# One looped copy in place of three nested copies of the code for an expert's further token blocks

## What is computed

```python
def moe_ffn(h, w_router, b_router, w_gate, w_up, w_down):
    expert, weight = group_limited_route(h, w_router, b_router)
    ...
    counts = jnp.bincount(e_flat, length=N_EXPERTS)
    padded = (counts + MOE_BLOCK - 1) // MOE_BLOCK * MOE_BLOCK
    ...
    def expert_block(args):
        tok, e = args
        xb = h[tok]
        return (jax.nn.silu(xb @ w_gate[e]) * (xb @ w_up[e])) @ w_down[e]
    y = lax.map(expert_block, (tok_buf.reshape(n_blocks, MOE_BLOCK), blk_exp))
```

## Time and profile before

| what | value |
|---|---|
| median of 3 runs | 1489.23 us (1488.87 to 1491.04) |
| span of the profiled execution | 1493.5 us |
| PE busy | 1380.9 us (92%), 7075 matmuls |
| DVE busy | 982.7 us (66%) |
| ACT busy | 726.7 us (49%) |
| experts of layer 0, of layer 1 | about 445 to 750 us, about 1137 to 1472 us |
| packets of the first instruction queue (q8) | 54, 0.88 MB |

### The profile page before, as it was taken

One profiled execution on the slowest core, in us unless ns is written; L12 is line 12 of the kernel. 1 busy time (PEld: TensorE's weight loads), 2 busy tenths in 40 slices (PEclk: granted clock), 3 DMA queues, 4 the chain that ended last, 5 costly groups with the idle time before them and its releaser, 6 DMA issues.

```text
span 1493.5 us, 18753 instructions
## 1 busy us (share of the span) xinstructions
PE 1380.9 (92%) x7075; PEld 1091.2 (73%) x7076; DVE 982.7 (66%) x934; ACT 726.7 (49%) x776; POOL 296.3 (20%) x255
## 2 busy tenths in 40 slices
PE   3999999999988999999949999999998899999893
PEld 1776877666866788888748787788777688888582
DVE  4324575323487899998971657632757889999285
ACT  4324355122254777766642635522325677776260
POOL 1000000000024344555310000000013435444130
PEclk9999999999999999999969999999998999999997
DMA  9766302776675999999743130132364899999365
GB/s 298 273 225 228 139 1 85 247 259 204 229 280 208 359 373 384 383 375 373 280 132 113 57 113 1 57 113 76 122 238 171 300 355 372 377 376 382 141 246 196
DMA packets 157267, 341.37 MB, mean 229 GB/s; under 512 B 17150, under 2 KB 19394, under 8 KB 157186
## 3 DMA queue, kind: packets, MB, share of 16 engines
q1 hardware_dynamic: 141170, 316.97, 58.7%
q0 software_dynamic: 16016, 23.30, 4.6%
HBM read 350.68 MB, written 23.61 MB: 251 GB/s over the span
## 4 chain that ended last, share of the span: by engine, by line
PE 76%; DVE 8%; DMA 6%; ACT 3%; DVEq 3%; issue 2%; SPq 2%; POOL 0%; ACTq 0%; POOLq 0%
PE PS L1185 15%; PE PS L1187 14%; PE PS L1186 14%; PE PS L1583 7%; PE PS L1587 7%; PE PS L1579 7%; PE PS L1119 3%; PE PS L1567 2%; DMA ring<-in_w_down 2%; ACT reg L939 1%; DVE ring_parts L2195 1%; DMA y_rows<-reg,icur 1%; PE PS L1592 1%; SPq L475 1%; DMA ring<-in_w_ada 1%
## 5 line engine op out<-in xcount | busy, mean ns | idle before, releaser
L1185 PE MATMUL PS<-ring_parts 128*128 128x512 f32 (+1 forms) x704 | 277.0, 393 | 8.8 <-DVE hT_parts L1827 5.1
L2195 DVE TENSOR_TENSOR ring_parts<-ring,reg_parts 128x2048 fp32r<-128x2048 f32 x124 | 278.2, 2285 | 7.5 <-ACT reg_parts L1043 7.4
L1043 ACT ACTIVATE reg_parts<-ring 128x2048 fp32r<-128x2048 f32 x124 | 230.6, 1909 | 82.3 <-DMA ring<-in_w_down 45.4
L1819 DVE TENSOR_TENSOR ring_parts<-ring,ring_parts 128x2048 fp32r<-128x2048 f32 (+1 forms) x52 | 112.9, 2210 | 153.9 <-ACT ring_parts L861 153.8
L1185 PEld LDWEIGHTS PS<-ring_parts 128*128 128x128 f32 x704 | 133.7, 190 | 60.1 <-issue 27.6
L861 ACT ACTIVATE ring_parts<-ring 128x2048 fp32r<-128x2048 f32 (+1 forms) x52 | 93.4, 1845 | 152.8 <-DMA ring<-in_w_in 113.9
L2195 DVE TENSOR_TENSOR ring_parts<-ring,hT_parts 128x2048 fp32r<-128x2048 f32 x68 | 155.3, 2289 | 11.1 <-issue 10.4
L1186 PE MATMUL PS<-hT_parts,ring_parts 128*128 128x512 f32 x384 | 150.4, 392 | 0.0
L1187 PE MATMUL PS<-ring_parts 128*128 128x512 f32 x384 | 150.4, 392 | 0.0
L1043 ACT ACTIVATE hT_parts<-ring 128x2048 fp32r<-128x2048 f32 x68 | 126.5, 1908 | 14.6 <-DMA ring<-in_w_gate 9.4
L1587 PE MATMUL PS<-ring_parts,reg_parts 128*128 128x512 f32 x528 | 130.6, 389 | 0.0
(11 more groups left out here) (328 smaller groups left out, 2398.6 us busy)
## 6 DMA issues: line engine op xcount, KB each, us to landing
ring<-in_w_up SPq DMA_DIRECT2D x32, 2048.0 KB, 17.4
ring<-in_w_gate SPq DMA_DIRECT2D x32, 2048.0 KB, 12.6
ring<-in_w_down SPq DMA_DIRECT2D x32, 2048.0 KB, 18.7
ring<-in_w_ada SPq DMA_DIRECT2D x40, 1024.0 KB, 5.3
ring<-in_w_in SPq DMA_DIRECT2D x16, 2048.0 KB, 7.8
ring<-in_w_ada SPq DMA_DIRECT2D x4, 2048.0 KB, 13.9
ring<-in_w_out SPq DMA_DIRECT2D x4, 2048.0 KB, 7.8
reg<-y_rows SPq DMA_DIRECT2D x16, 512.0 KB, 6.1
```

Of the source, the lines that this page charges most:

```text
L1043: act.activation(high[:, cols], ring[:, 3 * k + part, cols], ACT.Copy).then_inc(w_hi[part], 1)
L1185: pe.matmul(out_, left[0], right[0], start=first, stop=False)
L1819: tt(ring_r[:, unit_slot(n), cols], w, ring_r[:, 2 + n % 2, cols].bitcast(F32), ALU.subtract).then_inc(lo_done, 1)
L2195: tt(ring_r[:, 3 * k + part, cols], ring[:, 3 * k + part, cols], high[:, cols].bitcast(F32), ALU.subtract).then_inc(w_lo[part], 1)
```

## The change

`repeated_overflow_blocks` is new. It loads the count as before, tests once whether it is over 128, and inside that test runs a loop over b = 1, 2, 3 with b in a register; each pass compares the count with 128 b and runs `body` if it is larger. The code of `body` stands once at every call. PE, ACT and DVE call it; POOL keeps `overflow_blocks`. The bodies are unchanged: PE, ACT and DVE don't use the block's number.

```diff
+        def repeated_overflow_blocks(eng, e, done, body):
+
+            count = eng.value_load(cnt_i[0:1, bass.ds(e, 1)], min_val=0, max_val=SEQ)
+            with eng.If(count > P):
+                with eng.Fori(1, NT) as b:
+                    with eng.If(count > b * P):
+                        eng.reg_add(done, done, 1)
+                        body(None, eng.snap(done, min_val=1, max_val=4096))
+                        eng.nop()
+                eng.nop()
...
-                    overflow_blocks(act, e, done, body)
+                    repeated_overflow_blocks(act, e, done, body)
...
-                    overflow_blocks(pe, e, done, body)
+                    repeated_overflow_blocks(pe, e, done, body)
...
-                    overflow_blocks(dve, e, done, body)
+                    repeated_overflow_blocks(dve, e, done, body)
```

## The result

| | before | after |
|---|---|---|
| median of the runs of one comparison (16 each), us | 1491.72 (1486.74 to 1498.33) | 1485.45 (1481.22 to 1488.67) |
| ratio after to before | | 0.9946, 95% interval 0.9932 to 0.996 |
| the profiled execution: its time; span, us | as shown above; 1493.5 | 1481.74; 1480.1 |
| mean granted clock of TensorE in it | 0.969 | 0.973 |

The changed kernel is faster by 0.54%, which is 8.0 us (6.0 to 10.1). In all comparisons of this study together the kernel before has a mean of 1493.8 us over 103 runs and the changed kernel 1485.3 over 37: 8.5 us, with some 1.2 us either way from the spread of the runs (they come from several chips, so this is a summary and no comparison of its own).

What follows compares the result with a forecast made beforehand. PE, busy for 92% of the span, was taken as the bound. The terms 2.7 + 4.5 + 0.4 - 1.4 - 0.9 gave 5.3 us less, from 1489.2 to 1483.9 us; range 1481.5 to 1489.0.

Steps and rivals of the forecast that it cites:

- term (a): Ways around the bodies on PE in each layer's first steps: four holes go, 2.7 us less layer 0, 4.5 layer 1.
- of the window the trace disagrees: Loop over experts on PE: five blocks of code ran without one packet, against the skill's two-page window.
- term (b): Branch around the bodies in step 15 of layer 0, 4.9 us long: 0.4 us of its hold on PE go.
- term (c): Way out of expert 13's second block, layer 1: PE's remaining loop passes cost 1.4 us more (bounds 0.9 and 2.1).
- term (d): PE's clock behind expert 13's second block: longer idle may lengthen the low grant, 0.9 us more.
- Both cases that I named: Low-clock stretch behind expert 13's second block: 3.4 us longer, costing 1.7 us of work, or no longer, costing nothing.
- Weights take it back: In both layers PE's earlier start ends in waits for the down weights: 0.3 us less, 1488.9; chance 0.12.
- No effect on a first visit: A first visit costs a fetch however near the target; holes stay, way out is added: 1490.6 us; chance 0.07.
- The short loop misses its own code: After expert 13's block, four jumps of the further-block loop each cost a fetch: 7.9 us more, 1497.1; chance 0.08.

Runs made afterwards that it cites:

- Padding: The changed kernel with 308, 154 or 200 instructions behind PE's loop that never run; ratios to the kernel before 1.0028, 0.9988 and 0.9933.
- the engines one at a time: The changed kernel with the loop on PE alone, ratio to before 0.9953, or on ACT and DVE alone, 1.0008; the other engines keep three nested copies.
- the announced branch: The kernel before, with PE's branch around the bodies in steps 1 to 15 announced to the instruction fetch; 1490.85 us, ratio to before 0.998.
- 154 instructions never run: The changed kernel with 154 instructions behind PE's loop that a branch always skips; 1491.6 us, ratio to the kernel before 0.9988.
- the 308 run: The changed kernel with 308 instructions behind PE's loop that a branch always skips; 1496.59 us, ratio to the kernel before 1.0028.
- The six passes: The changed kernel with block numbers 1 to 6 in the loop in place of 1 to 3; 1489.9 us, ratio to the kernel before 0.9973.
- the counted loop: The changed kernel with the loop's end worked out once from the count, without comparisons inside; 1481.04 us, ratios to before 0.9921, 0.9926, 0.993.
- 200 never run: The changed kernel with 200 instructions behind PE's loop that a branch always skips; 1483.69 us, ratio to the kernel before 0.9933.

## Why the prediction was right, and where it was short

**The holes, term (a).** Right in cause and place. All four are gone, q8 brought 44 packets as forecast, no branch is over 0.35 us. Padding, the engines one at a time and, in layer 1, the announced branch show that it is the block in which the branch lands, and not the number of copies. The wording needs one correction: a target one block ahead is not free in itself (up to 2.2 us of branch with 154 instructions never run, and 2.4 with a hole of 1.4 at step 2 of layer 0 before); it is mostly short enough for PE's queue.

The Trainium skill (Runtime: NRT & Kernel Launch, Instruction fetch mechanics) forces a fetch where the target of a taken branch is outside a two-page window. For a first visit the runs agree in the main: 0.2 to 2.4 us of branch at one block ahead, 3.3 us and more at two. For code visited before they don't: the loops of this study, up to five blocks long, ran on without a packet. The same section also gives TensorE an instruction memory of 2048 instructions, eight of these blocks, in which such a loop fits. So the prediction's "of the window the trace disagrees" holds against the section's two pages, and not against that figure; no run here has a loop long enough to test it.

The size was short. I let 2.7 + 4.5 = 7.2 us through; the steps gained 3.5 + 4.9 = 8.4 in the profiled pair. Two things were off there. The idle time in the rows is less than what a hole costs the steps, 7.4 against 8.4: the missing 1.0 us stands in no wait of the list, and what it is (shorter waits, a slower start behind a hole) stays open. And I kept 0.2 us back for the weights, which took nothing: from step 4 to step 15 of layer 0 the other kernels take 194.8 to 195.4 us whether they have holes or not (before itself 196.0), although ACT still gets the down weights 18.6 us apart (before 18.37):

```profile
666.50 3.73 ACT L1054 ACTIVATE reg_parts<-ring 128x2048 fp32r<-128x2048 f32 x2 [3.39 <-DMA ring<-in_w_down]
...
685.13 3.73 ACT L1054 ACTIVATE reg_parts<-ring 128x2048 fp32r<-128x2048 f32 x2 [2.71 <-DMA ring<-in_w_down]
```

In the other kernels with the long branches in layer 0 the first steps there cost 3.7 to 4.4 us more than the 50.0 of all kernels without, so 3.5 is at the low end.

**Step 15, term (b).** I had 0.4 us. From the tokens of step 15 to the first product of `last_down` layer 0 takes 26.3 to 27.1 us in the four profiles with the 4.9 us branch and 25.4 to 26.4 in the nine with a branch of 0.35 us at most: 0.9 on average, with ranges that touch. I had counted only the 0.44 us behind DVE's last part.

**The way out, term (c).** Right: 1.4 forecast, 1.5 measured, 2.1 us between DVE's end and PE's restart forecast, 2.19 measured. The six passes and the counted loop show that PE's empty passes are it. My sum for the added passes was built from the earlier trace rows, and 0.75 us a pass bears it out.

**The clock, term (d).** 0.9 forecast; 1.3 in the profiled pair (5.9 against 3.4 us of work at the lower level), about 1.4 over all profiles. Both cases that I named occur: the three profiles of the changed kernel have 5.9, none and 3.4 us. The prediction took 0.9 as the middle of two guesses, so that it lies near is in part luck.

**The sum.** With the measured sizes it is 3.9 (the mean of the nested layout's and the 308 run's first steps in layer 0) + 4.8 + 0.9 - 1.5 - 1.4 = 6.7 us, against 5.3 forecast and 8.0 (6.0 to 10.1) measured. What is between 6.7 and 8.0 I can't place; it is inside the interval. The predicted time, 1483.9, lies 1.6 below the median of 1485.45, and the range held it. That is partly luck: the median of three runs from which I started, 1489.2, was low (1491.7 over 16 runs, 1493.5 over all 103), by 2.5 us or more, while the gain that I took off it was 2.7 too small. Ratios would have been the safer forecast: 0.9964 against 0.9946.

**The rivals.** Weights take it back: no, see above. No effect on a first visit: no, by the packets and the branches. The short loop misses its own code: no; from 1212 to 1430 us, the second block and the way out included, after has no q8 packet at all, and the instruction queues show only this:

```profile
q14 instruction: 2, 0.02, 0.0%
```

The length between the layers, which the forecast didn't touch, is what separates single profiles: 396 to 403 us from the first product of `last_down` in layer 0 to layer 1's first tokens, in kernels with and without holes alike. Of the 13 us between the first two profiles 4.3 come from there, and go with the mean grant of 0.95 against 0.97.

## What to carry to other kernels

Code that is skipped nearly always still costs when the branch around it leaves the block of code under way and the next: here some 472 instructions of it, 1.85 blocks of 256, cost TensorE 8.4 us of 1490 in the first steps of the two layers, with no engine and no transfer behind the holes. Look at the sequencer's branch records first, lay the stream out in blocks, and make the skipped part short or its target lie at most one block ahead (and not near that block's end, as the targets at 25.86 and 48.96 show); the number of instructions alone says little. When copies become a loop, work out its end once, so that no engine leaves it through empty passes while all others wait: it took the idle time from 3.44 to 1.70 us.

## What the runs showed of the hardware that I had not expected

- 46 instructions more in the skipped part made the kernel 0.5% faster (154 against 200 never run, 0.9988 against 0.9933): the targets moved by a fraction of a block, and the holes of layer 0 went.
- The same branch took 0.9 us with its target at block 48.96 and 4.0 us at 49.00, with the same hole behind it.
- An announced branch was followed by its fetch about 4 us later in layer 1 and at step 15, and by none in layer 0's first steps; and it cost 3.9 us elsewhere, at a branch within the bodies that had been free.
- A pause of TensorE some 1.5 us longer was followed by 3.5 us of work at the lower clock on average instead of 0.7 (seven and five profiles, with a wide spread).
